# The last residual addition of a two-layer decoder step, moved from VectorE into accumulating DMAs on the output

## The reference

```
def _rmsnorm(x, g):
    xf = x.astype(jnp.float32)
    y = xf * lax.rsqrt(jnp.mean(xf * xf, axis=-1, keepdims=True) + NORM_EPS)
    return (y * g.astype(jnp.float32)).astype(x.dtype)

def _mlp(h, w1, w2):
    a = jax.nn.relu(h @ w1)
    return (a * a) @ w2
...
        xp = xp + _rmsnorm(mp, gn[1])
        xs = xs + _rmsnorm(ms, gn[1])
        xp = xp + _rmsnorm(_mlp(_rmsnorm(xp, gn[2]), w_ff1[layer], w_ff2[layer]), gn[3])
        xs = xs + _rmsnorm(_mlp(_rmsnorm(xs, gn[2]), w_ff1[layer], w_ff2[layer]), gn[3])
    return (xp, xs,
```

## Time and profile before

| | |
|---|---|
| runs without profile, median (range) | 984.0 us (983.85 to 984.16) |
| profiled execution, its own time | 984.47 us |
| span of the profiled execution | 982.5 us |
| TensorE busy | 961.2 us, 98% of the span |
| VectorE busy | 594.3 us, 60% |
| ScalarE busy | 432.1 us, 44% |
| GpSimd busy | 37.6 us, 4% |
| last TensorE matmul of the last product, start | 970.9 us |
| VectorE's last scaling and addition | 973.8 to 980.0 us |

### The profile page before, as it was taken

One profiled execution on the slowest core, in us unless ns is written; L12 is line 12 of the kernel. 1 busy time (PEld: TensorE's weight loads), 2 busy tenths in 40 slices (PEclk: granted clock), 3 DMA queues, 4 the chain that ended last, 5 costly groups with the idle time before them and its releaser, 6 DMA issues. The chain is left out here.

```text
span 982.5 us, 17788 instructions
## 1 busy us (share of the span) xinstructions
PE 961.2 (98%) x7572; PEld 889.4 (91%) x7572; DVE 594.3 (60%) x770; ACT 432.1 (44%) x545; POOL 37.6 (4%) x68
## 2 busy tenths in 40 slices
PE   8999999999999999999999999999999999999996
PEld 8988998757999999999997988788899899999996
DVE  6866654666586564344785767676674775543443
ACT  6232224676655443333542544434444565443331
POOL 0510000000000000000001010000000000000000
PEclk9999999999999999999999999999999999999998
DMA  9988759856344444444546878674674255444421
GB/s 344 372 278 277 267 192 357 306 196 245 129 172 171 160 158 159 167 171 171 207 177 236 296 259 293 232 291 182 250 279 156 108 205 171 171 165 155 159 78 48
DMA packets 50990, 206.63 MB, mean 210 GB/s; under 512 B 3568, under 2 KB 3952, under 8 KB 35440
## 3 DMA queue, kind: packets, MB, share of 16 engines
q1 hardware_dynamic: 45504, 182.58, 52.4%
q0 software_dynamic: 5424, 23.15, 6.0%
HBM read 181.39 MB, written 24.33 MB: 209 GB/s over the span
## 5 line engine op out<-in xcount | busy, mean ns | idle before, releaser
L1284 ACT ACTIVATE wH<-raw 128x2048 fp32r<-128x2048 f32 x115 | 220.3, 1916 | 351.9 <-PE banks L631 344.3
L1676 DVE TENSOR_TENSOR wL<-raw,wH 128x2048 fp32r<-128x2048 f32 x112 | 256.5, 2291 | 192.6 <-ACT wH L1284 192.6
L629 PE MATMUL banks<-hH,wH 128*128 128x288 f32 x1216 | 365.9, 301 | 2.5 <-DVE hL L1685 1.2
L631 PE MATMUL banks<-hH,wL 128*128 128x288 f32 x1216 | 358.6, 295 | 0.0
L630 PE MATMUL banks<-hL,wH 128*128 128x288 f32 x1216 | 358.4, 295 | 0.0
L629 PEld LDWEIGHTS banks<-hH,wH 128*128 128x128 f32 x1216 | 229.8, 189 | 17.5 <-issue 10.7
L630 PEld LDWEIGHTS banks<-hL,wH 128*128 128x128 f32 x1216 | 228.8, 188 | 1.1 <-issue 0.7
L631 PEld LDWEIGHTS banks<-hH,wL 128*128 128x128 f32 x1216 | 228.5, 188 | 0.0
L631 PE MATMUL banks<-aH,wL 128*128 128x288 f32 x512 | 151.8, 296 | 0.0
L629 PE MATMUL banks<-aH,wH 128*128 128x288 f32 x512 | 151.3, 296 | 0.0
L630 PE MATMUL banks<-aL,wH 128*128 128x288 f32 x512 | 149.3, 292 | 0.0
(11 more groups left out here) (302 smaller groups left out, 1024.7 us busy)
## 6 DMA issues: line engine op xcount, KB each, us to landing
raw<-wst SPq DMA_DIRECT2D x119, 1024.0 KB, 4.9
cache_sb<-kcache SPq DMA_DIRECT2D x14, 1024.0 KB, 7.5
sslot<-state SPq DMA_DIRECT2D x11, 1024.0 KB, 5.6
sstate_out<-sslot POOLq DMA_DIRECT2D x11, 1024.0 KB, 5.9
raw<-vcache SPq DMA_DIRECT2D x6, 1024.0 KB, 9.9
w_area<-vcache SPq DMA_DIRECT2D x6, 1024.0 KB, 12.8
raw<-state SPq DMA_DIRECT2D x5, 1024.0 KB, 5.3
sstate_out<-raw POOLq DMA_DIRECT2D x5, 1024.0 KB, 5.5
```

The costliest lines, as they stand in the source:

```text
L629: nc.tensor.matmul(out[:, m, :], wH[:, u % 2, c], hi[:, k, :], start=first, stop=False)
L631: return nc.tensor.matmul(out[:, m, :], wL[:, u % 2, c], hi[:, k, :], start=False, stop=last)
L1284: nc.scalar.activation(wH[:, at % SPL, :], raw[:, raw_slot(at), :], ACT.Copy).then_inc(h_round, 1)
L1676: nc.vector.tensor_tensor(wL[:, at % SPL, :], raw[:, raw_slot(at), :], wH[:, at % SPL, :].bitcast(F32), ALU.subtract).then_inc(l_split, 1)
```

## The change

The last residual's addition no longer runs on VectorE. `x` as it stands after residual 2 is stored to `x_out` as a whole (1152 KB) by a DMA in POOL's list, after the last `pstate_out`. At the end VectorE only scales the four groups of `y`, and for each of them POOL issues a DMA from `y` to `x_out` with `accum_op=ALU.add`, so that the DMA engines add to what lies in HBM. SP's four stores are gone; POOL and SP wait for `fin`.

```
@@ SyncE's list @@
             strips(S_RETOUT + N_RETOUT, N_STRIPS)
-            for k, n in X_LAST:
-                sp.wait_ge(x_done, 3 * KT + k + n)
-                sp.dma_start(x_out[:, k:k + n, :], x[:, k:k + n, :]).then_inc(fin, 16)
             sp.wait_ge(fin, 16 * len(X_LAST))
@@ GpSimd's list @@
             store_prompt_state(NHR - 1)
+            pool.wait_ge(x_done, 3 * KT)
+            pool.dma_start(x_out, x[:, :, :]).then_inc(x_stored, 16)
             pool.wait_ge(k_stored, 16)
...
             for j in range(U_SLOTS):
                 pool.wait_ge(s_stored[j], 16 * (6 if j == 0 else 5))
+
+            pool.wait_ge(x_stored, 16)
+            for k, n in X_LAST:
+                pool.wait_ge(t_done, 3 * KT + k + n)
+                pool.dma_start(x_out[:, k:k + n, :], y[:, k:k + n, :], accum_op=ALU.add).then_inc(fin, 16)
+            pool.wait_ge(fin, 16 * len(X_LAST))
@@ VectorE's list, residual() @@
                     nc.vector.tensor_tensor(y[:, c, :], y[:, c, :], rs, ALU.mult).then_inc(t_done, n)
                     for i in behind:
                         split_x(b, i, nlayer, nnorm)
+                    if b is None:
+                        continue
                     dve.wait_ge(t_done, KT * e + k + n)
                     nc.vector.tensor_tensor(x[:, c, :], x[:, c, :], y[:, c, :], ALU.add).then_inc(x_done, n)
-                    behind = range(k, k + n) if b is not None else ()
+                    behind = range(k, k + n)
```

More of the change, by code:

```diff
@@ L384, in build_program @@
         relu_sq, a_round, a_split = map(sem, ("relu_sq", "a_round", "a_split"))
-        fin = sem("fin")
+        fin, x_stored = sem("fin"), sem("x_stored")
         half_round, half_split = sem("half_round"), sem("half_split")
```

## The result

The changed kernel takes 990.2 us (median of 4 runs, 989.9 to 990.5) against 984.0 us before: the ratio is 1.0064, with a 95% interval of 1.0051 to 1.0076. The change makes the kernel 6.2 us slower. The forecast was 984.7 us and no change that can be measured; the time lies in the stated range of 981.3 to 991, near its upper end and on the side that had a chance of 0.40, and outside the likeliest case's own 982.0 to 986.0.

The account below looks back on a forecast made before the run. TensorE bounds the kernel, VectorE then the store its tail. First byte 975.64 + 4 x 1.54 accumulating + 0.5 extra read + 0.9 to end = 983.2 span; plus 1.97, less 0.47 without profile: 984.7 us, range 981.3 to 991.

Parts of the forecast that it names:

- the side that had a chance of 0.40: Whole kernel: slower by over 0.2%, from a DMA-engine-bound accumulate (0.30), POOL's issues as bound (0.08) or delayed strips (0.02).
- the likeliest case: Tail: an accumulate costs two reads at full rate, 0.88 to 1.87 us per group; 984.7 us as the value, chance 0.45.
- VectorE's 3.4 us: Tail: without four additions of 0.76 us and four gaps of 0.09 us, VectorE is done 3.40 us earlier.
- The early store costs nothing: From 776 us: storing x (3.1 us of the DMA engines) costs 0, covered by 9 us of slack; 3.1 at most otherwise.
- GpSimd keeps up: Tail: an accumulating issue on POOL takes about 0.55 us like a plain one, less than VectorE's 0.68 us between groups.
- The rule weighed: Tail: by the skill, VectorE's two-port modes keep GpSimd from writing descriptors, so issues could wait for scalings; counted as 0.
- The rival of issues as the bound: Tail: accumulating issues on POOL take longer, passing the forecast from 1.3 us each, deciding from 1.6; 987.5 us at 2; chance 0.08.
- D: Tail: time one accumulated group occupies the DMA engines, 1.54 us, twice a plain store's 0.77.
- The rival of a slow adder: Tail: read, read and write don't overlap or the adder is slow; 2.3 us per group, 987.8 us; chance 0.30.
- 0.9 us to the end: Very end: from the last byte, 0.5 us until the store counts as landed and 0.4 until the span ends.
- the serial case: Tail: each group a load then a store, nothing overlapped, 4.6 us each; 995.2 us; within the chance of 0.30.
- the sign that I had named myself: Tail: the forecast is wrong if from 976.6 us to the end takes under 4 us or over 9.

Follow-up runs that it names:

- the plain kernel: The changed kernel with plain stores of y on GpSimd in place of the accumulating DMAs, GpSimd's last wait kept, last addition left out of the output: 984.7 us.

## Why the prediction was wrong where it was

- **What bounds the kernel** held: only the tail moved. Up to the first scaling of the last residual the two profiled executions differ by 0.38 us, the changed one being ahead.
- **VectorE's 3.4 us**: right. Measured alone 3.2 us.
- **The early store costs nothing**: right, measured alone at 1.0000.
- **GpSimd keeps up**: wrong as stated, without a cost. An accumulating issue takes 0.88 us and not 0.55, more than VectorE's 0.68, so GpSimd falls behind; its issues do not bound, because the DMA engines take longer still. The rule weighed on VectorE holding up GpSimd's issues does not show: plain issues beside the scalings take 0.54 us. But the first one starts 0.58 us after the scaling, where I had put nothing, and the first byte comes 1.3 us after it instead of 1.1. Bytes start 2.62 us after the first scaling's start; the sum had 1.88. That is 0.7 us. The rival of issues as the bound is out: at 0.88 us per issue it stays under the 1.3 us from which it would pass the sum. Longer issues alone, which I had named as its sign, do not show it.
- **D, the cost of accumulating**: the step was mis-sized. I had 1.54 us per group from two reads at full rate; the engines were busy for 1.93. With the stragglers the bytes last 9.0 us (976.0 to 985.0), where the sum had 4 x 1.54 + 0.5 = 6.7: 2.3 us more. The step that failed is the factor 2 on the row of a plain store; measured it is 2.5. That the engines read each byte twice was an assumption from the start, and no row counts a second read (the page has 181.39 MB read from HBM before and after). The rival of a slow adder had D = 2.3; the measured 1.93 passes the 1.87 from which it was to decide, and lies between the two. The Trainium skill (Collectives: The Full Stack, Why ReduceScatter is half of AllGather) gives 1/1.93 of the rate for a sum of two sources against a copy; here an accumulate has 1/2.5 of a plain store's rate into HBM and 1/2.2 into SBUF, so this case shows more than that rule gives.
- **"0.9 us to the end"**: this step failed, and no rival had it. I carried SyncE's distance from last byte to end over to a kernel in which GpSimd waits too, and wrote only that both wait for `fin`. It is 3.6 us, 2.7 more, and the drain of 2.27 us could be read in the trace before, at 778.1, under the closing line, which I had not read.

**The range held, and that was in part luck.** Its upper end, 991, came from half of the serial case, and the groups did not run one after the other (that kernel takes 997.9 us). What brought the time to 990.2 was mostly an accumulate dearer than two reads and a drain that the range did not know. By the sign that I had named myself the forecast fails: from the last scaling (976.1) to the end it is 12.5 us, over the 9 that I had set.

The three together, 0.7 + 2.3 + 2.7 = 5.7, and the 0.7 us that I had forecast make 6.4 of the tail's 6.5 us. By runs without profile: -3.2 (VectorE) + 2.5 (the way through GpSimd) + 1.3 (its last wait) + 5.5 (accumulating) = 6.1 us. Both sums must come out, since their terms are the steps of one chain of times; what they show is how large each step is. The drain's step depends on the order: 1.3 us taken off the plain kernel, 1.7 off the changed one, 2.3 put on the kernel before. Even without the last wait, the step that no rival had, the change would have been slower (988.5 us).

What stays open: why an add in the DMA engines takes 2.2 times a plain store even between two places in SBUF. Two reads would make it 2 if reading bounds, which no run shows; what the second read, the adding and the description of the transfer each have in it, no run here parts. Nor is it shown why two or three engines trail by 2 us with four accumulates into HBM and not with two longer ones or into SBUF.

## What to carry to other kernels

When work moves to another engine's queue at the end of a program, read that engine's closing lines as well: a drain that was hidden in mid-program becomes part of the time once something late is put on its list. Price an accumulating DMA like these (288 or 576 KB, rows of 2304 or 4608 bytes) at 2.2 to 2.5 plain stores of the same bytes, and remember that every other store in flight shares the engines with it. In the last microseconds of this kernel, where the end waits for its result, it did not pay. Whether it pays where the DMA engines idle and nobody waits, no run here shows.

## What the runs showed of the hardware that was not expected

- GpSimd's closing drain takes 2.27 us with its DMAs long landed, 2.68 us in the kernels that store late through its queue and wait for it, and ends 1.3 to 1.4 us behind the last landing when it starts early (10.48 us long in one kernel). Behind GpSimd's own additions it ends 2.3 us after the last. SyncE's takes 7 ns.
- GpSimd's first store of the tail is issued 0.6 us after its releaser, plain or accumulating, and a plain one starts its bytes 1.1 us after issue; SyncE's figures are 0.03 and 0.85 us. GpSimd's first addition follows its releaser by 0.18 us.
- Accumulating DMAs move 160 GB/s where plain stores move 383 (295 KB in 0.77 us), and two in flight raise the landing of SyncE's stores from 2.1 to 4.8 us.
- Issuing an accumulating DMA holds GpSimd for 0.83 to 0.89 us, a plain one of the same bytes for 0.54.
- A VectorE addition with both operands in SBUF takes 1.11 us instead of 0.76 when it starts during a GpSimd addition, and 0.76 when it starts just before one, which then takes 1.91 us instead of 1.40.
